# Turning the hidden rows of a feed-forward block: 32x32 blocks on VectorE and a gather through DRAM in place of TensorE's transposes

## The reference, cut to what matters

```
def sq_relu_mlp(h, w1, w2):                      # h 256 x 2048, w1 2048 x 8192, w2 8192 x 2048
    return jnp.square(jax.nn.relu(h @ w1)) @ w2
```

## Time and profile before

| | |
|---|---|
| median of 3 runs | 2822.73 us (2822.43 to 2824.7) |
| the profiled execution | 2820.31 us |
| its span, first to last instruction | 2818.7 us |
| `mlp1` | about 343 to 1075 us of the span |
| `mlp2` | about 2094 to 2805 us of the span |

### The profile page before, as it was taken

How to read it: one execution, slowest core, us unless ns; L and a number is a source line. 1 busy time by engine, 2 the same in 40 slices (tenths; PEclk the granted TensorE clock), 3 DMA queues, 4 the chain that set the end, 5 groups by cost and what they waited for, 6 DMA issues and landing times.

```text
span 2818.7 us, 34529 instructions
## 1 busy us (share of the span) xinstructions
PE 2782.9 (99%) x12939; PEld 2314.6 (82%) x12939; DVE 1997.9 (71%) x2268; ACT 1374.9 (49%) x1719; POOL 146.9 (5%) x109
## 2 busy tenths in 40 slices
PE   9999999999999999999999999999989999999998
PEld 7887888888888888788888888898878888888887
DVE  5666877899997676757785488687975467754455
ACT  5446454443443455557444445754554444344443
POOL 0000010010000100000000001000001000010010
PEclk9999999999999999999999999999999999999999
DMA  8963887888888777555666666408855588775654
GB/s 256 215 203 108 279 277 267 280 273 284 287 277 309 260 252 234 196 194 171 217 192 198 198 182 186 134 6 309 307 183 182 193 276 275 255 202 190 191 186 157
DMA packets 332780, 623.09 MB, mean 221 GB/s; under 512 B 37015, under 2 KB 38807, under 8 KB 330903
## 3 DMA queue, kind: packets, MB, share of 16 engines
q1 hardware_dynamic: 323543, 601.52, 66.8%
q10 hardware_dynamic: 9088, 19.56, 1.9%
HBM read 614.68 MB, written 7.27 MB: 221 GB/s over the span
## 4 chain that ended last, share of the span: by engine, by line
PE 93%; DVE 3%; DMA 2%; ACT 1%; issue 1%; SPq 0%; DVEq 0%; POOLq 0%; POOL 0%; ACTq 0%
PE ps L1400 86%; DMA raw<-w_in 1%; PE ps L1379 1%; PE ps L1610 1%; PE ps L1813 1%; PE ps L1793 1%; DMA raw<-w_o 1%; PE ps L1421 1%; DVE wlo L1936 1%; PE ps L1831 1%; PE ps L1532 0%; ACT whi L706 0%; PE ps L1512 0%; DVE macc L2142 0%; DVE cf L2291 0%
## 5 line engine op out<-in xcount | busy, mean ns | idle before, releaser
L1936 DVE TENSOR_TENSOR wlo<-raw,whi 128x1024 fp32r<-128x1024 f32 x940 | 1168.5, 1249 | 731.3 <-ACT whi L706 726.8
L706 ACT ACTIVATE whi<-raw 128x1024 fp32r<-128x1024 f32 x939 | 994.9, 1060 | 1222.6 <-PE ps L1400 1111.2
L1400 PE MATMUL ps<-whi,hhi 128*128 128x512 f32 x2032 | 549.5, 392 | 1.5 <-DVE yrow L2159 1.5
L1400 PE MATMUL ps<-whi,hlo 128*128 128x512 f32 x2032 | 544.0, 389 | 0.0
L1400 PE MATMUL ps<-wlo,hhi 128*128 128x512 f32 x2032 | 543.4, 389 | 0.2 <-DVE wlo L1936 0.2
L1400 PEld LDWEIGHTS ps<-wlo,hhi 128*128 128x128 f32 x2032 | 381.4, 188 | 80.1 <-DVE wlo L1936 0.6
L1400 PEld LDWEIGHTS ps<-whi,hlo 128*128 128x128 f32 x2032 | 381.1, 188 | 79.7
L1400 PE MATMUL ps<-whi,xhi 128*128 128x512 f32 x1632 | 442.7, 393 | 1.6 <-issue 1.6
L1400 PEld LDWEIGHTS ps<-whi,hhi 128*128 128x128 f32 x2032 | 378.3, 188 | 79.5 <-DVE yrow L2159 1.9
L1400 PE MATMUL ps<-whi,xlo 128*128 128x512 f32 x1632 | 440.1, 392 | 0.0
L1400 PE MATMUL ps<-wlo,xhi 128*128 128x512 f32 x1632 | 437.8, 390 | 0.0
(11 more groups left out here) (312 smaller groups left out, 1476.6 us busy)
## 6 DMA issues: line engine op xcount, KB each, us to landing
raw<-w_in SPq DMA_DIRECT2D x296, 512.0 KB, 4.4
raw<-mlp_w SPq DMA_DIRECT2D x256, 512.0 KB, 3.8
mraw<-w_mod SPq DMA_DIRECT2D x384, 256.0 KB, 5.0
raw<-w_up SPq DMA_DIRECT2D x128, 512.0 KB, 4.6
raw<-w_down SPq DMA_DIRECT2D x128, 512.0 KB, 4.9
raw<-w_o SPq DMA_DIRECT2D x32, 512.0 KB, 5.3
raw<-w_ple_gate SPq DMA_DIRECT2D x32, 512.0 KB, 3.7
raw<-w_out SPq DMA_DIRECT2D x32, 512.0 KB, 5.9
```

Of the source, the lines that this page charges most:

```text
L706: nc.scalar.activation(whi[:, s % NSLOT], raw[:, s % NSLOT], ACT.Copy).then_inc(hi_done, 1)
L1400: ins = nc.tensor.matmul(ps[:, bank(par) + th], a[:, kt, th * P:(th + 1) * P], b[:, (s + u) % NSLOT, k], start=(kt == 0 and m == 0), stop= ...
L1936: nc.vector.tensor_tensor(wlo[:, s % NSLOT], raw[:, s % NSLOT], whi[:, s % NSLOT].bitcast(F32), ALU.subtract)\
```

## The change: 15 of the 32 turns by another way

For groups `c` = 0, 1, 2 of every block of `mlp2`, and of the last block of `mlp1` (`by_blocks`, 12 + 3 = 15 groups), PE no longer transposes. Instead, in the chunk after the group's:

- DVE slot 2 (`blocks_turned`): wait for the squares, then two 128x512 transposes in 32x32 blocks from `sqrow` into `hturned`, which has the place of `rrow`;
- ACT slot 3 (`blocks_out`): wait for them, then one DMA of 512 KB to the DRAM tensor `hidden_blocks`;
- ACT slot 5 (`blocks_in`): wait until that has landed, then four DMAs of 128 KB, each into 32 partitions of `hgather` (the place of `sqrow`) in runs of 1 KB;
- ACT slot 7 (`blocks_high`): wait for the four, then two copies of 128x512 into `hhi`;
- DVE slot 7 (`blocks_low`): after each copy, the subtraction into `hlo`; its end frees `sqrow` for POOL.

Group `c` = 3 is turned by PE as before. Some semaphores are shared to make room for the new ones (`early_in` and `gqk_in` become `tables_in`; `e_out` and `e_in` join `spill` and `reload`), and POOL's two loops over the blocks are written out.

```
+        hturned = at("hturned", [P, STACK, TH, STACK, BLK], F32, work_at + 32 * K)
+        hgather = at("hgather", [P, STACK, TH, STACK, BLK], F32, work_at + 36 * K)
+        hidden_blocks = nc.dram_tensor("hidden_blocks", (P, STACK, TH * STACK * BLK), F32, kind="Internal").ap()
...
+        def by_blocks(k, i, c):
+            return c < 3 and (k == "mlp2" or i == NSB - 1)
...
 ACT:
+                        def blocks_out(c=j - 1, i=i):
+                            n = VIA.index((k, i, c))
+                            act.wait_ge(ht_done, n + 1)
+                            act.dma_start(hidden_blocks, hturned[:].rearrange("p g t k b -> p g (t k b)")).then_inc(ht_out, 16)
+                        def blocks_in(c=j - 1, i=i):
+                            n = VIA.index((k, i, c))
+                            act.wait_ge(ht_out, 16 * (n + 1))
+                            for g in range(STACK):
+                                src = bass.AP(hidden_blocks.tensor, g * TH * STACK * BLK,
+                                              [[STACK * TH * STACK * BLK, BLK], [BLK * STACK * TH * STACK * BLK, STACK], [1, TH * STACK * BLK]])
+                                act.dma_start(hgather[BLK * g:BLK * (g + 1)].rearrange("p i t k b -> p i (t k b)"), src).then_inc(ht_in, 16)
+                        def blocks_high(c=j - 1, i=i):
+                            n = VIA.index((k, i, c))
+                            act.wait_ge(ht_in, 16 * STACK * (n + 1))
+                            for th in range(TH):
+                                nc.scalar.activation(hhi[:, 4 * c:4 * c + 4, th * P:(th + 1) * P].rearrange("p k (i b) -> p k i b", b=BLK),
+                                                     hgather[:, :, th].rearrange("p i k b -> p k i b"), ACT.Copy).then_inc(t_hi, 1)
...
-                              extra=merge(extras.get(len(SEQ) * i + j, {}), {TURN_U: turned} if j and SEQ[j - 1][0] == "U" else {}))
+                              extra=merge(extras.get(len(SEQ) * i + j, {}), {} if j < 1 or j > 4 else
+                                          {3: blocks_out, 5: blocks_in, 7: blocks_high} if by_blocks(k, i, j - 1) else {TURN_U: turned}))
...
 PE:
-                              inserts=merge(extras.get(n, {}), {3: turn_hidden} if j and SEQ[j - 1][0] == "U" else {}, sum_inserts(k, n)),
+                              inserts=merge(extras.get(n, {}), {3: turn_hidden} if 1 <= j <= 4 and not by_blocks(k, i, j - 1) else {}, sum_inserts(k, n)),
...
 DVE:
+                        def blocks_turned(c=j - 1, i=i):
+                            dve.wait_ge(sq_done, i * 8 + 2 * (u0 + c) + 4)
+                            for th in range(TH):
+                                ins = nc.vector.transpose(hturned[:, :, th], sqrow[:, th].rearrange("p (k g b) -> p g k b", k=STACK, g=STACK))
+                            ins.then_inc(ht_done, 1)
+                        def blocks_low(c=j - 1, i=i):
+                            for th in range(TH):
+                                dve.wait_ge(t_hi, i * 8 + (h0 + 2 * c + th + 1))
+                                cs = slice(th * P, (th + 1) * P)
+                                nc.vector.tensor_tensor(hlo[:, 4 * c:4 * c + 4, cs].rearrange("p k (i b) -> p k i b", b=BLK),
+                                                        hgather[:, :, th].rearrange("p i k b -> p k i b"),
+                                                        hhi[:, 4 * c:4 * c + 4, cs].rearrange("p k (i b) -> p k i b", b=BLK).bitcast(F32),
+                                                        ALU.subtract).then_inc(t_free, 1)
...
-                                          {TURN_U: turned} if j and SEQ[j - 1][0] == "U" else {}))
+                                          {} if j < 1 or j > 4 else {2: blocks_turned, 7: blocks_low} if by_blocks(k, i, j - 1) else {TURN_U: turned}))
...
 POOL:
-                            pool.wait_ge(t_done, i * 8 + (TG[k][0] + 2 * c))
+                            if c and by_blocks(k, i, c - 1):
+                                pool.wait_ge(t_free, TG[k][0] + 8 * i + 2 * c)
+                            elif c:
+                                pool.wait_ge(t_done, hidden_turned(k, i, c - 1, 1))
+                            else:
+                                pool.wait_ge(t_done, TG[k][0] + 8 * i)
...
-            with pool.Fori(0, NSB) as i:
+            for i in range(NSB):
                 mlp(i, "mlp2")
```

More of the change, by code:

```diff
@@ L308, in build @@
         small_in = sem("small_in")
-        early_in = sem("early_in")
+        tables_in = sem("tables_in")
         x_in = [sem(f"x_in{n}") for n in range(len(X_PARTS))]
@@ L325, in build @@
         bias_done = sem("bias_done")
-        gqk_in = sem("gqk_in")
         gqk_done = sem("gqk_done")
@@ L351, in build @@
         lb_exp = sem("lb_exp")
-        e_out = sem("e_out")
-        e_in = sem("e_in")
+        ht_done = sem("ht_done")
+        ht_out = sem("ht_out")
         lb_out = sem("lb_out")
+        ht_in = sem("ht_in")
         lb_rows = sem("lb_rows")
@@ L556, in build, with skipped, hidden_turned @@
             tc = [tc[0] + groups, tc[1] + groups * counted]
+        def by_blocks(k, i, c):
+            return c < 3 and (k == "mlp2" or i == NSB - 1)
+        VIA = [(k, i, c) for k in ("mlp1", "mlp2") for i in range(NSB) for c in range(4) if by_blocks(k, i, c)]
+        def skipped(k, i, c):
+            return 2 * sum(by_blocks(k, i, b) for b in range(c))
+        def hidden_turned(k, i, c, h):
+            return TG[k][0] + 8 * i + 2 * c + h + 1 - (skipped(k, i, c) if c < 3 else 0)
         block = ctx.enter_context(nc.Block())
@@ L774, in spread_gains @@
             def spread_gains():
-                act.wait_ge(gqk_in, 32)
+                act.wait_ge(tables_in, 48)
                 for n, (a, b) in enumerate(((0, A_Q), (A_Q, NA))):
@@ L1122, in _ @@
                     if c == 10:
-                        act.wait_ge(spill, 16)
+                        act.wait_ge(spill, 32)
                     f = half_evac(urow, c, g)
@@ L1314, in row_squares @@
             def row_squares(th):
-                act.wait_ge(reload, 16)
+                act.wait_ge(reload, 32)
                 act.wait_ge(merged, 4)
@@ L1611, in turn_hidden @@
                                                                   sqrow[:, th, f:f + P], ident)
-                                ins.then_inc(t_done, 1)
+                                ins.then_inc(t_done, 1 + (skipped(k, i, c) if c == 3 and h == 0 else 0))
                         def hidden(u, i=i):
-                            return (lambda: pe.wait_ge(t_hi, i * 8 + (TG[k][1] + u + 1))), (lambda: pe.wait_ge(t_free, i * 8 + (t0 + u + 1)))
+                            m = i * 8 + (u // 2 * 2 + 2 if by_blocks(k, i, u // 2) else u + 1)
+                            return (lambda: pe.wait_ge(t_hi, TG[k][1] + m)), (lambda: pe.wait_ge(t_free, t0 + m))
                         st = (xhi, xlo) if kind == "U" else (hhi, hlo)
@@ L2034, in squares @@
                         dve.wait_ge(gqk_done, 1)
-                        dve.wait_ge(early_in, 16)
+                        dve.wait_ge(tables_in, 48)
                     step(nc.vector.tensor_tensor(ra, pj, pj, ALU.mult))
@@ L2273, in _ @@
             d_first = c_first + 32
-            mlp("mlp1", place({0: lambda: post0_res(3), 1: low1(3), 2: low1(4), 3: low1(5), 4: low1(6), 5: low1(7), 6: norm1_mean_square,
+            mlp("mlp1", 0, place({0: lambda: post0_res(3), 1: low1(3), 2: low1(4), 3: low1(5), 4: low1(6), 5: low1(7), 6: norm1_mean_square,
                                c_first + 5: mod_of_mixer, c_first + 6: mixer_gains,
@@ L2321, in gated @@
                 dve.wait_ge(acc_free, plan["gate"][1] + c + 3)
-                dve.wait_ge(e_in, 16)
+                dve.wait_ge(reload, 16)
                 cs = slice(c * NCH, (c + 1) * NCH)
@@ L2559, in post3_gain @@
                     dve.wait_ge(gb_out, 16)
-                    dve.wait_ge(reload, 16)
+                    dve.wait_ge(reload, 32)
                     dve.wait_ge(merged, 4)
@@ L2618, in _ @@
             last = 8 * (len(SEQ) * NSB - 4)
-            mlp("mlp2", place({0: lambda: [low4(0), norm4_row(2)], 1: lambda: [low4(1), norm4_row(3)],
+            mlp("mlp2", 16, place({0: lambda: [low4(0), norm4_row(2)], 1: lambda: [low4(1), norm4_row(3)],
                                **{g: (lambda g=g: low4(g)) for g in range(2, 8)}, 137: last_mods, **{last + 8 * c + 13: (lambda c=c: post4_gain(c)) for c in range(3)}}))
```

15 lines of the change are left out of this document (8 added, 7 removed).

## The result

The changed kernel takes 2829.09 us (median of 12 runs, 2826.25 to 2830.73), the kernel before on the same chips 2822.22 (12 runs): a ratio of 1.0026, with a 95% interval of 1.0018 to 1.0033. It is slower by some 7 us, where 2810 was forecast. The profiled execution has a span of 2827.3 us.

A forecast was written before the change was run, and what follows sets the result against it. PE was taken to pace the kernel: the profiled 2820.31 us, less 13.4 for removed turns, plus 0.7 for the column, gave 2807.6; with the runs' median 2.42 above the profile, 2810.0. The 8-in-10 range was 2807 to 2820.

The forecast's parts named there:

- What is removed: PE's turns in the 15 changed groups: each costs PE 0.89 us, so removing them saves 13.4 us.
- Rival 1: PE's turns: each transpose costs its recorded 0.272 us, so 15 turns save 32.6 us, giving 2790; chance 0.02.
- What is added: DVE transposes, DRAM write, gathers and copies, followed through one crowded chunk: split ends at 24.0 us, margin 3.2 us.
- The price of all this on the end is therefore nothing: Added work in the changed chunks: costs the end nothing, hidden behind the three pieces ACT and DVE work ahead.
- S: Sum of the two landings, DRAM write and gathers, in a changed group: taken as 10.3 us.
- Rival 3: DRAM round trip lands late everywhere: with S 15, five blocks lose 42 us, giving 2852; chance 0.13.
- 11 + S: Loop from one group to the next, in us: relu, squares, transposes, issues, copies, split and landings, against a 21.77 us chunk.
- Traffic, charged at nothing: DMA in changed chunks: 1 MiB more each, 48 GB/s, charged nothing since the context load passed 331 GB/s without stalling PE.
- The column's charge of 0.7 us: Groups around the column written element by element: DMA make-up delays weights, charged 0.7 us, between 0 and about 8.
- rival 2: DMA crowding in part of the groups: seven stall 0.5 to 1.5 us each, 4 to 10 us, 2813 to 2820; chance 0.18.

The follow-up runs named there:

- Six quiet groups: The change only in the six groups of mlp2's blocks 0 and 3, where only weights are streamed, against the kernel before: 2817.74 us, ratio 0.9984.
- the 12 late groups: The change in mlp2's twelve groups only, copies and subtractions moved to slots 2 and 3 of the chunk after, against the kernel before: 2812.35 us, ratio 0.9964.
- the first experiments: Four choices of changed groups against the kernel before: none 2822.68 us, mlp2 blocks 0 and 3 2817.74, mlp1 block 3 plus mlp2 block 1 2836.35, mlp1 block 3 2828.79.
- the kernel without the trip: The change in mlp1 block 3 and mlp2 block 1 only, without DRAM write, gathers or their waits, against the kernel before: 2820.12 us, ratio 0.9998.
- run 313: Not a run label: "run" is a verb here, and 313 GB/s is the DMA rate of one of two stretches without an idle us on PE.
- e1_none: All other edits of the change, but all 32 groups turned on PE as before, against the kernel before: 2822.68 us, ratio 1.0003.
- e5_b3: The change only in the three groups of mlp1's block 3, against the kernel before: 2828.79 us, ratio 1.0034.
- e7_late_all: All 15 groups changed, copies and subtractions moved to slots 2 and 3 of the chunk after, against the kernel before: 2810.29 us, ratio 0.9966.
- six crowded ones: As a late run: mlp1 block 3 and mlp2 block 1 only, copies and subtractions in the chunk after, against the kernel before: 2818.60 us, ratio 0.9989.
- e3_crowded: The change only in the six groups of mlp1's block 3 and mlp2's block 1, copies at slot 7, against the kernel before: 2836.35 us, ratio 1.0053.

## Why the prediction was wrong, point by point

**What is removed: right.** 136 of 256 transposes are left, and chunks of 21.77 us came out wherever nothing waited. Six quiet groups gave 4.5 us for 5.3, the 12 late groups 10.2 for 10.7. Rival 1 is out: a removed turn gave 0.89 us, not 2.2, though the line of the turns (durations in ns: minimum, median, maximum) still records 272 for a transpose, as in the earlier trace rows:

```profile
L1648 PE MATMUL ps<-small,sqrow x136: 270/272/472, 388.2 to 2739.8; 128*128 128x128 f32 x136
```

**What is added, term by term.** Transposes 2 x 0.683, forecast 2 x 0.68. Issues 0.34 for the write and 4 x 0.45 for the gathers, forecast 0.6 and 2.4. The write lands after 5.6 us in the median, the last gather after 7.2, forecast 4.3 and 6.0 from the earlier trace rows. Those rows count from the issue, so the forecast counted two issues twice, which hid part of the error: from the write's issue to the last landing it had 13.3 us, and the 15 groups took 12.5 to 17.2.

**The step that failed: "The price of all this on the end is therefore nothing".** It rested on following one chunk, and on one S of 10.3 for all groups in the loop to the next. The one chunk came out nearly so: in the first group of block 1 the split behind the copies ends 20.3 us after the squares, forecast 19.5. The loop didn't. S is 12.9 and 13.0 in the two rounds of `mlp2` shown above (4.47 + 8.38, 4.78 + 8.21) and 14.0 to 15.6 in `mlp1`. The prediction gave the point where lateness builds up as S over 10.8 and the one where the saving is lost as about 13. The first was passed in every group, since S is 11.2 to 14.2 in the nine others of `mlp2` too. The second was wrong: at 13.0 block 1 lost its saving and 3.4 us more, while block 3 of `mlp2`, with S of 12.4 to 13.0, kept its 2.7 us. So S doesn't tell block 1 from the blocks that won, and the theory of the first experiments, that the trip is late only where DMA is full, is not borne out there. What tells it apart is the next term. Rival 3 worked the loop out, but with one S for all groups as well, and without that term.

**A second term, in the loop.** It was written as 11 + S. The timeline of the changed kernel in block 1 gives what a late group really meets on VectorE between squares and transposes; behind it, a round of block 3, where only weights are streamed:

```profile
2333.47 2.98 DVE L2181 SCALAR_TENSOR_TENSOR macc<-mraw,cols,macc 128x512 f32<-128x512 f32 x2
2336.38 2.35 DVE L1975 TENSOR_TENSOR wlo<-raw,whi 128x1024 fp32r<-128x1024 f32 x2
2338.65 1.53 DVE L2181 SCALAR_TENSOR_TENSOR macc<-mraw,cols,macc 128x512 f32<-128x512 f32 x2
2340.09 1.30 DVE L2246 STREAM_TRANSPOSE hturned<-sqrow 128x512 f32<-128x512 f32 x2
...
2341.87 2.01 ACT L723 ACTIVATE whi<-raw 128x1024 fp32r<-128x1024 f32 x2 [5.73 <-DVE hturned L2246]
```

```profile
2689.16 3.10 POOL L2740 TENSOR_TENSOR sqrow<-rrow 128x512 f32<-128x512 f32 x2 [19.22 <-ACT rrow L940]
2693.26 1.29 DVE L2246 STREAM_TRANSPOSE hturned<-sqrow 128x512 f32<-128x512 f32 x2
2694.58 0.34 ACTq L911 DMA_DIRECT2D hidden_blocks<-hturned  x1
2708.90 1.16 ACT L925 ACTIVATE hhi<-hgather 128x512 fp32r<-128x512 f32 x2 [3.95 <-DMA hgather<-hidden_blocks]
2712.05 3.09 POOL L2740 TENSOR_TENSOR sqrow<-rrow 128x512 f32<-128x512 f32 x2 [19.79 <-ACT rrow L940]
```

The squares that start at 2333.35 (above) end at 2335.91, the transposes start at 2340.09: 4.2 us in which VectorE does modulation products and `wlo`, which the loop had at nothing. The round is then 2.56 squares, 4.18 of VectorE's queue, 1.30 transposes, 4.78 write, 1.3 to the last gather's issue, 8.21 gather, 3.2 for copies, split and relu: 25.5, and the squares are 25.56 apart. Against the forecast of 21.3 (S of 10.3), S brings 2.7, the queue 4.2, and the other terms together give back 2.7, of which 1.7 are the issues. The round of block 3 has the same trip, 14.3 us from the write's issue to the copies, but 1.0 us between squares and transposes, and takes 22.9. So in block 1 the queue makes the difference between a group that wins and one that loses. In block 3 of `mlp1` both terms are larger: 2.1 us on VectorE for the late groups, and a trip of 15.4 to 17.2. This is read from the trace; no run takes the modulation products out of a crowded block. That the queue alone doesn't lose is shown by the kernel without the trip, where the transposes of block 1 come 2.45 us after the squares and the chunks take 21.76.

**Traffic, charged at nothing: right at this size.** The two stretches above run 313 and 324 GB/s without an idle us on PE. How near the limit is stays open: a further 512 KB a group cost 5.4 us in all, but with a longer wait.

**The column's charge of 0.7 us: not separated.** The chain runs through one round of block 2 (landings 5.63 and 6.72), and PE's timetable gains 1.4 us in that block where 2.7 were to be had; no run isolates it.

**A loss that was in no step: the context stage behind `mlp1`.** It takes longer in every kernel whose block 3 of `mlp1` was changed. Two starts, a small turn behind `mlp1` and a product at the end of the stage, first where none of the groups was changed (`e1_none`):

```profile
1075.96 0.60 PE L1606 MATMUL ps<-small,macc 128*128 128x128 f32 x4
1197.77 1.02 PE L1691 MATMUL ps<-lfc,sums 128*128 128x512 f32 x2
```

and with the three groups of `mlp1` alone (`e5_b3`):

```profile
1080.58 0.60 PE L1606 MATMUL ps<-small,macc 128*128 128x128 f32 x4
1205.06 1.02 PE L1691 MATMUL ps<-lfc,sums 128*128 128x512 f32 x2
```

That is 121.8 and 124.5 us. It is 119.9 in the kernel before and 121.7 and 121.8 in the two others that leave `mlp1` alone; it is 123.1 to 125.5 in all ten that change it, whether the block ended early (no trip, late copies) or late. So the stage doesn't merely take back a gain: the changed kernel loses there as well. PE's time from the last turn of a block to that of the next, in us, puts the parts side by side:

| | before | `e1_none` | changed kernel | `e7_late_all` |
|---|---|---|---|---|
| `mlp1`, block 2 to 3 | 178.6 | 178.6 | 184.6 | 175.9 |
| the stage behind it | 119.9 | 121.8 | 123.9 | 123.9 |
| `mlp2`, block 0 to 1 | 177.7 | 177.7 | 181.1 | 175.0 |
| block 1 to 2 | 178.2 | 178.2 | 176.8 | 175.5 |
| block 2 to 3 | 177.7 | 177.7 | 175.1 | 175.0 |

Late copies give 2.7 us in every block, as forecast. The stage is why 15 late groups give no more than 12, and six crowded ones 3.1 us instead of 5.3. What makes it longer was not tried and stays open.

**The rivals.** What happened is rival 2 in its place (part of the groups, those with the modulation matrix) with the mechanism of rival 3 (the loop over the round trip). Rival 2 names nine groups and prices seven at 0.5 to 1.5 us; against the forecast the six crowded ones cost PE 2.0 us each in block 1 and 2.9 in block 3 of `mlp1`, and the three around the column 0.4. The two chances of 0.18 and 0.13 were kept apart, as if a case had to hold everywhere or stay small; together with the six crowded groups' weight they should have been the main question. That the quiet groups won as forecast, although their S was 11.2 to 14.2 and not 10.3, is luck in part: the lead of three pieces covered what the sum had too small.

## What to carry to other kernels

Price a transfer that an in-order engine waits for by the last landing that ends the wait, in the stretch where it runs, and not by the median of single transfers; and close the loop from one group to the next with every task that the late engine finds queued ahead. If the result isn't wanted soon, wait for it one stage later: here the same bytes cost nothing once the wait stood three slots, some 8 us, further on. Measure the stage behind a changed one as well: here it lost 1.3 to 3.7 us more, for a reason that stays open.

## What the runs showed of the hardware that was not expected

**A short stall can cost twice.** In block 3 of `mlp1` PE stood 2.39 us, and the products after it ran slower. Stretches, then PE's timeline, both of the changed kernel:

```profile
960.00:967.00 7.00, 4.71 (x21) 3.57 (x19) 1.29 (x2) 2.05 (x4) 0.00 (x0) 1.00 1.06 321
967.00:970.30 3.30, 3.20 (x9) 2.50 (x10) 3.19 (x3) 3.30 (x6) 2.03 (x2) 0.59 0.36 106
```

```profile
967.10 1.69 PE L1438 MATMUL ps<-whi,xhi 128*128 128x512 f32 x4 [2.39 <-ACT whi L723]
968.58 1.91 PE L1438 MATMUL ps<-whi,xlo 128*128 128x512 f32 x4
970.29 1.42 PE L1438 MATMUL ps<-wlo,xhi 128*128 128x512 f32 x4
971.54 1.07 PE L1438 MATMUL ps<-whi,xhi 128*128 128x512 f32 x4
```

The granted clock is 0.59 in the 3.3 us after the stall, so most of it is at the 1.2 GHz level. The 12 products from 967.10 to 971.54 take 4.44 us where 12 x 0.2267 is 2.72: 1.7 us on top of the 2.39. A second stall there did the same (0.73). In block 1 of `mlp2`, with 1.16 us idle of the 7.90 from 2350, the clock stayed at 1.00. So it did after longer stalls in other runs: 2.79 us at 968.5 in `e3_crowded` and 2.90 us at 992.8 in `e5_b3` were each followed by 3.3 us at 1.00. The length of a stall alone doesn't decide it.

**A transfer to DRAM landed no sooner for being 16 times shorter** beside full DMA engines: 5.4 us for 32 KB in 512 packets, 5.6 for 512 KB in 128.
